# A hybrid mixing and MoE layer step: expert outputs summed in PSUM, scaled selections, nine staged weight slots

## The reference, cut to what matters

```python
x = x + mix
x = x + moe(rmsnorm(x, norm_ffn_g), w_router, b_router, w_up, b_up, w_down, b_down)
...
gu = xb @ w_up[e] + b_up[e]
gate, up = gu[:, :D_EXPERT], gu[:, D_EXPERT:]
act = (up + 1.0) * (gate * jax.nn.sigmoid(SWIGLU_ALPHA * gate))
return act @ w_down[e] + b_down[e]
...
y = jax.ops.segment_sum(out * row_gate[:, None].astype(out.dtype), row_tok, num_segments=n_tok)
```

## Time and profile before

| what | value |
|---|---|
| median of 3 runs | 1290.15 us (1289.37 to 1290.32) |
| span of the profiled execution (the only time given for it) | 1288.5 us |
| PE busy | 1174.2 us (91%) |
| DVE busy | 605.2 us (47%) |
| POOL busy | 467.4 us (36%) |
| ACT busy | 249.7 us (19%) |
| moved by DMA | 448.97 MB, 348 GB/s over the span |

### The profile page before, as it was taken

One profiled execution on the slowest core, in us unless ns is written; L12 is line 12 of the kernel. 1 busy time (PEld: TensorE's weight loads), 2 busy tenths in 40 slices (PEclk: granted clock), 3 DMA queues, 4 the chain that ended last, 5 costly groups with the idle time before them and its releaser, 6 DMA issues.

```text
span 1288.5 us, 30593 instructions
## 1 busy us (share of the span) xinstructions
PE 1174.2 (91%) x11113; PEld 577.5 (45%) x11114; DVE 605.2 (47%) x1256; ACT 249.7 (19%) x487; POOL 467.4 (36%) x833
## 2 busy tenths in 40 slices
PE   8999999999999899798979998989989799899876
PEld 7777777775434333233323433433333233233232
DVE  2999983122644344354343442444524244444243
ACT  2012124001222122122212221212211122122112
POOL 1022300000444435445451454454444444535451
PEclk9999999999999999999989999999999999999997
DMA  9983442344899999999998799999999999999996
GB/s 260 337 269 119 144 135 105 129 155 166 334 385 399 421 421 422 421 421 421 422 421 364 307 398 422 420 422 421 422 421 421 421 421 421 422 421 408 421 421 254
DMA packets 94570, 448.97 MB, mean 348 GB/s; under 512 B 8526, under 2 KB 42894, under 8 KB 45339
## 3 DMA queue, kind: packets, MB, share of 16 engines
q1 hardware_dynamic: 93742, 446.55, 86.5%
q10 hardware_dynamic: 749, 1.19, 0.3%
q0 software_dynamic: 48, 0.85, 0.2%
HBM read 447.00 MB, written 2.42 MB: 349 GB/s over the span
## 4 chain that ended last, share of the span: by engine, by line
PE 55%; DMA 15%; DVE 13%; POOL 6%; issue 6%; SPq 3%; ACT 1%; DVEq 0%; POOLq 0%; ACTq 0%
PE banks L1369 20%; DMA ring<-in_w_down 15%; PE banks L1379 12%; DVE R L800 8%; PE banks L1164 8%; POOL ring L530 6%; PE banks L1086 4%; PE banks L1144 3%; PE banks L1123 2%; PE banks L1280 2%; SPq L398 1%; PE banks L1130 1%; PE banks L1153 1%; DVE R L809 1%; DVE R L812 0%
## 5 line engine op out<-in xcount | busy, mean ns | idle before, releaser
L1369 PE MATMUL banks<-ring,hT 128*32 128x512 f32 x3328 | 430.4, 611 | 62.3 <-POOL ring L530 57.5
L530 POOL COPY ring<-big 128x512 f32<-128x512 f32 x248 | 146.9, 641 | 554.4 <-SPq L404 554.4
L530 POOL COPY ring<-R 128x512 f32<-128x512 f32 x496 | 289.9, 631 | 113.4 <-DMA R<-in_w_up 113.4
L321 DVE TENSOR_TENSOR xt<-xt,banks 128x1024 f32<-128x1024 f32 x106 | 128.7, 1215 | 403.7 <-PE banks L1144 403.7
L1379 PE MATMUL banks<-ring,hT 128*32 128x256 f32 x3328 | 227.4, 392 | 18.4 <-DMA ring<-in_w_down 13.2
L1379 PEld LDWEIGHTS banks<-ring,hT 128*32 128x32 f32 x3328 | 107.5, 113 | 202.8 <-issue 123.3
L1164 PE MATMUL banks<-hT,ring 128*128 128x288 f32 x768 | 189.2, 407 | 0.2 <-ACT hT L554 0.2
L1369 PEld LDWEIGHTS banks<-ring,hT 128*32 128x32 f32 x3328 | 95.5, 111 | 195.6 <-POOL ring L530 81.1
L1164 PEld LDWEIGHTS banks<-hT,ring 128*128 128x128 f32 x768 | 145.7, 191 | 39.9 <-issue 0.3
L680 ACT COPY WT<-banks 128x256 f32<-128x256 f32 x52 | 19.4, 373 | 498.2 <-PE banks L1379 498.2
L800 DVE SCALAR_TENSOR_TENSOR R<-big,convw,R 128x256 f32<-128x256 f32 x240 | 108.1, 525 | 0.0
(11 more groups left out here) (252 smaller groups left out, 757.2 us busy)
## 6 DMA issues: line engine op xcount, KB each, us to landing
ring<-in_w_down SPq DMA_DIRECT2D x128, 1024.0 KB, 11.0
R<-in_w_up SPq DMA_DIRECT2D x124, 1024.0 KB, 18.1
ring<-in_w_up SPq DMA_DIRECT2D x70, 1024.0 KB, 9.4
big<-in_w_up SPq DMA_DIRECT2D x62, 1024.0 KB, 12.7
ring<-in_w_in SPq DMA_DIRECT2D x24, 1024.0 KB, 10.3
ring<-in_w_branch_b SPq DMA_DIRECT2D x4, 1024.0 KB, 4.9
ring<-in_w_branch_a SPq DMA_DIRECT2D x4, 1024.0 KB, 4.9
ring<-in_w_out SPq DMA_DIRECT2D x4, 1024.0 KB, 4.9
```

Of the source, the lines that this page charges most:

```text
L321: nc.vector.tensor_tensor(dst, dst, rows, ALU.add).then_inc(y_added, 1)
L530: ins = nc.gpsimd.tensor_copy(ring[:, k, h * 512:(h + 1) * 512], parked[k][:, h * 512:(h + 1) * 512])
L1369: ins = mm(UP[g * BLK:(g + 1) * BLK, :], xT[:, k, :], ring[:, k, g * 512:(g + 1) * 512], start=k == 0, stop=k == UP_SLOTS - 1)
```

## The change

It does five things.

- The sums of all expert outputs for rows 0 to 255 stay in four PSUM banks (`total`) from the first item to the last. `clear_total` opens them once with matmuls of zeros before the loop; every combine accumulates (`start=False`), and DVE adds the two totals to `xt` once after the loop. The last item's output still goes the old way (`tail_out`). The sample rows are added per body as before.
- PE gathers from `xt` itself; the selections carry each row's scale instead of 1. The scaled copy in `stage` goes. The sum of squares of rows 0 to 255 comes from statistics on DVE (`bn_stats`, `bn_aggr`) instead of a square on ACT.
- The buffers of the mixing part move into one region, `arena`, laid out so that nine parked slots fit: up 0 to 7 and the first down slot.
- Before the loop SP loads five parked slots once the spatial gating has been taken out of PSUM (`sp_evac`), a sixth after the first four slots of the first expert, two after `ya_evac` and the ninth at the end.
- In the loop SP releases nine slots, loads three directly, and takes turns in another order (`next_weights`). POOL makes 36 copies per expert instead of 24.

Constants for the order of experts are made on POOL after the convolution instead of near the start, in a buffer that is free only then. The diff, cut to its core:

```diff
-PARKED = 6
+PARKED = 9
+EARLY_SLOTS = 5
+ARENA = PARKED * SLOT + D
...
+        arena = sb("arena", [P, ARENA])
+        parked = [arena[:, k * SLOT:(k + 1) * SLOT] for k in range(PARKED)]
+        stage = region(NT * D).rearrange("p (t d) -> p t d", t=NT)
+        spb = region(G * P).rearrange("p (g i) -> p g i", g=G)
+        big = region(KC * CB)
...
+        region(EARLY_SLOTS * SLOT - taken[0])
+        R1, R2, R4, R3 = (region(KC * T) for _ in range(4))
+        fing = arena[:, PARKED * SLOT:PARKED * SLOT + D]
...
+        zeros = comb[:, 0].rearrange("p q j -> p (q j)")
...
-        row_out = (high[:, :, 0:256], high[:, :, 256:512])
+        total = (high[:, :, 0:256], high[:, :, 256:512])
...
+            def wait_used(k, before):
                 if k < UP_SLOTS:
+                    sp.wait_ge(up_used, before * UP_SLOTS + (k + 1))
                 else:
+                    sp.wait_ge(down_used, before * DOWN_SLOTS + (k - UP_SLOTS + 1))
+            def release_parked(before, ks):
+                for k in ks:
+                    wait_used(k, before)
                     sp.sem_inc(released, 1)
+            def load_direct(e, before, ks):
+                for k in ks:
+                    wait_used(k, before)
                     load_slot(e, k)
...
+            sp.wait_ge(sp_evac, 2 * G)
+            sp.wait_ge(v_stored, 16)
+            for k in range(EARLY_SLOTS):
+                load_parked(1, k)
             for k in range(UP_SLOTS):
                 sp.wait_ge(*mix_block_used(MIX_BLOCKS - SLOTS + k))
                 load_slot(0, k)
+                if k == 3:
+                    load_parked(1, EARLY_SLOTS)
             sp.wait_ge(ya_evac, 2 * KC)
-            for k in range(PARKED - 1):
+            for k in range(EARLY_SLOTS + 1, PARKED - 1):
                 load_parked(1, k)
             for k in range(UP_SLOTS, SLOTS):
                 sp.wait_ge(*mix_block_used(MIX_BLOCKS - SLOTS + k))
                 load_slot(0, k)
             load_parked(1, PARKED - 1)
             sp.wait_ge(before_known, 1)
+            def next_weights(place, here, after, before):
+                release_parked(before, range(0, 3))
+                load_parked_again(place + 1, after, (0,))
+                release_parked(before, (3,))
+                load_parked_again(place + 1, after, (1,))
+                release_parked(before, (4,))
+                load_parked_again(place + 1, after, (2,))
+                release_parked(before, (5, 6))
+                load_parked_again(place + 1, after, (3,))
+                release_parked(before, (7,))
+                load_parked_again(place + 1, after, (4,))
+                release_parked(before, range(UP_SLOTS, PARKED))
+                load_direct(here, before, range(PARKED, SLOTS))
+                load_parked_again(place + 1, after, range(5, PARKED))
             with sp.Fori(1, NE - 1) as place:
                 before = sp.value_load(items_before[0:1, bass.ds(place - 1, 1)], min_val=0, max_val=MAX_ITEMS)
                 here = sp.value_load(order[0:1, bass.ds(place, 1)], min_val=0, max_val=NE - 1)
                 after = sp.value_load(order[0:1, bass.ds(place + 1, 1)], min_val=0, max_val=NE - 1)
-                release_parked(before)
-                load_up_rest(here, before)
-                load_parked_again(place + 1, after, range(0, 2))
-                load_down(here, before)
-                load_parked_again(place + 1, after, range(2, PARKED))
+                next_weights(place, here, after, before)
             before = sp.value_load(items_before[0:1, NE - 2:NE - 1], min_val=0, max_val=MAX_ITEMS)
             here = sp.value_load(order[0:1, NE - 1:NE], min_val=0, max_val=NE - 1)
-            release_parked(before)
-            load_up_rest(here, before)
-            load_down(here, before)
+            release_parked(before, range(PARKED))
+            load_direct(here, before, range(PARKED, SLOTS))
...
-                nc.scalar.activation(stage[:, tt, :], xt[:, tt, :], ACT.Square, accum_out=ss[:, tt:tt + 1]
...
-                for tt in range(NT):
-                    ins = V.tensor_scalar(sel[:, tt, :], slot_ids[:, bass.ds(rank0, BLK)],
-                                          rankm[:, tt, bass.ds(expert, 1)], None, ALU.is_equal)
-                ins.then_inc(sel_ready, 1)
+                for tt in range(2):
+                    V.tensor_scalar(sel[:, tt, :], slot_ids[:, bass.ds(rank0, BLK)],
+                                    rankm[:, tt, bass.ds(expert, 1)], ss[:, 4 + tt:5 + tt], ALU.is_equal, ALU.mult)
+                V.tensor_scalar(sel[:, 2, :], slot_ids[:, bass.ds(rank0, BLK)],
+                                rankm[:, 2, bass.ds(expert, 1)], None, ALU.is_equal).then_inc(sel_ready, 1)
...
+                dve.wait_ge(x2_ready, 2 * tt + h + 1)
+                link(V.bn_stats(bnst[:, tt, h, :], dst))
+                if h == 1:
+                    link(V.bn_aggr(mv[:, tt, :], bnst[:, tt, :, :]))
+                    V.scalar_tensor_tensor(ss[:, tt:tt + 1], mv[:, tt, 0:1], mv[:, tt, 0:1], mv[:, tt, 1:2],
+                                           ALU.mult, ALU.add).then_inc(squared2, 1)
...
-                if tt < 2:
-                    V.tensor_scalar(stage[:, tt, :], xt[:, tt, :], col2, None, ALU.mult).then_inc(rows_kept, 1)
...
-            dve.wait_ge(combined, 1)
-            add_output(dve, row_out[0], 0)
...
-            def add_before(i, tt):
-                dve.wait_ge(combined, i * NT + (tt + 1))
-                add_output(dve, row_out[tt], tt) if tt < 2 else add_quarters(dve, DN[:, 256:512])
+            def add_before(i):
+                dve.wait_ge(combined, i + 1)
+                add_quarters(DN[:, 256:512]).then_inc(y_added, 1)
             with dve.Fori(0, bodies) as i:
                 column, column1, column2 = (
...
                 activate(i, column)
                 take_x(i + 1)
                 swish(i)
-                add_before(i, 2)
+                add_before(i)
                 dve.wait_ge(combT_turned, i + 1)
                 select_weighted(column1)
                 dve.wait_ge(gathered, i + 2)
                 select(column2)
-                add_before(i, 1)
-                dve.wait_ge(combined, i * NT + (NT + 1))
-                add_output(dve, row_out[0], 0)
...
-            add_before(bodies, 2)
-            add_before(bodies, 1)
+            add_before(bodies)
+            for tt in range(2):
+                add_rows(total[tt], tt).then_inc(total_added, 1)
...
-                    mm(XB[q * BLK:(q + 1) * BLK, 0:256], sel[:, tt, :], stage[:, tt, q * 256:(q + 1) * 256],
+                    mm(XB[q * BLK:(q + 1) * BLK, 0:256], sel[:, tt, :], xt[:, tt, q * 256:(q + 1) * 256],
...
+            def clear_total():
+                for q in range(QN):
+                    row = slice(q * BLK, (q + 1) * BLK)
+                    mm(high[:, q, :].rearrange("p (h n) -> p h n", h=2), zeros[row, :],
+                       slot_ids[row, 0:256].unsqueeze(1).to_broadcast([BLK, 2, 256]), start=True, stop=False)
-                             out_sb[q * BLK:(q + 1) * BLK, :], start=True, stop=True)
+                             out_sb[q * BLK:(q + 1) * BLK, :], start=start, stop=stop)
...
-                pe.wait_ge(y_added, i * NT + 1)
-                combine(1, row_out[1])
+                combine(1, total[1], False, stop)
...
                     pe.wait_ge(listed, 1)
+                    clear_total()
                     tr(DN[0:1, 0:P], item_column).then_inc(list_turned, 1)
...
-            combine(0, row_out[0])
+            combine(0, total[0], False, False)
...
-                combine_before(i)
+                combine_before(i, False)
                 turn_weights(i)
                 pe.wait_ge(xT_ready, i + 2)
                 for k in range(UP_SLOTS):
                     up(k, after)
                     if k == 1:
                         pe.wait_ge(act_ready, i + 1)
-                        pe.wait_ge(y_added, i * NT + 2)
+                        pe.wait_ge(y_added, i + 1)
                     if 1 <= k <= DOWN_SLOTS:
                         down(k - 1, here)
                     if k == 6:
                         pe.wait_ge(combT_ready, i + 2)
                         pe.wait_ge(out_ready, i + 1)
-                        pe.wait_ge(y_added, i * NT + NT)
-                        combine(0, row_out[0])
+                        combine(0, total[0], False, False)
...
-            pe.wait_ge(y_added, bodies * NT + NT)
+            pe.wait_ge(total_added, 2)
...
```

More of the change, by code:

```diff
@@ L134, in hybrid_layer, with region @@
-        rank_at = sb("rank_at", [NE, NE - FIXED])
-        movable = sb("movable", [NE, 1])
-        first_place = sb("first_place", [NE, 1])
-        big = sb("big", [P, KC * CB])
-        R1 = sb("R1", [P, KC * T])
-        R2 = sb("R2", [P, KC * T])
-        R3 = sb("R3", [P, KC * T])
-        R4 = sb("R4", [P, KC * T])
+        stageq = sb("stageq", [P, 256])
+        fingq = sb("fingq", [P, 256])
```

(57 more changed lines are left out.)

126 lines of the change are left out of this document (49 added, 77 removed).

## The result

The changed kernel takes 1366.84 us (median of 4 runs, 1363.16 to 1370.85) against 1289.76 for the kernel before: a ratio of 1.0602, interval [1.0586, 1.0618]. It is slower by 77 us. The prediction said 1280.4 and gave "slower" a chance of 0.10.

A forecast was written before the change was run, and what follows sets the result against it. The prediction took the DMA stream of expert weights as the bound. Its terms, -7.5 - 3.6 - 1.5 + 0.4 + 2.5 = -9.7 us, gave span 1278.8 and time 1280.4 us, range 1266 to 1288.

The forecast's parts named there:

- POOL beside DVE: DVE's activation work under POOL's longer copying: one slower body per expert, five experts pay; +2.5 us, bounds 0 and 8.
- rival C: Four DVE operations of the activation chain each wait out one whole copy: 1.6 us a body, time 1285.9; chance 0.08.
- Only the five experts in the stretches that PE holds pay: Part of the +2.5 us for DVE under copies: the slower body costs time only where PE holds the stream back.
- Rival D: Between turned rows and first down, a 2.5 us delay in every body makes PE the bound: 1300; chance 0.06.
- Rival B: SP's loads: late POOL copies hold up every load behind them, gaps grow and the gain goes: 1290; chance 0.10.
- Start of the stream: The loop's first load waits only for POOL's copy of slot 0, so bytes flow from 336.8: -3.6 us.
- Gaps: Stream runs dry at direct loads in early cycles and around the three-block expert: losses 20.2 against 21.7, -1.5 us.
- Last byte: End of the weight stream: the last byte lands at 1260.1, 12.6 us earlier.
- Adds, clearing, routing, selections: Adds removed from DVE, totals cleared on PE, routing statistics on DVE, scaled selections: 0 each, clearing's 1.3 us counted in cycles.
- The end: Work behind the last weight byte: nothing is shortened; +0.4 us, at most +0.9, at least 0.

The follow-up runs named there:

- the ninth run: The changed kernel, with POOL waiting for its own copies after the third and sixth slot of an expert only; 1282.50 us, 0.9949 of the kernel before.
- the fourth run: The changed kernel, with DVE's multiply for the next block's xT moved ahead of the clamp of the gate; 1346.01 us, 1.0430 of the kernel before.
- the third run: The changed kernel with six slots staged, not nine, and the old order of loads, the rest kept; 1289.17 us, 0.9998 of the kernel before.

## Why the prediction was wrong

**The step that failed is "POOL beside DVE": +2.5 us, bounds 0 and 8.** It took its price from the one body of the earlier trace rows whose activation lay under copies, 0.5 us, and its upper bound from one whole copy per conflict (rival C). Both assume that DVE gets its turn when a copy ends. The body seen had 13 copies behind its clamp, which was 0.58 us long:
```profile
344.01 0.58 DVE L1026 TENSOR_SCALAR hT<-hT 128x256 f32<-128x256 f32 x1
```
It was not the only one: 26 of that kernel's 52 clamps begin under a copy, most behind 1 to 4, and none takes over 0.77 us. The price of a short wait was about right; but no clamp of the kernel before stood behind 15 copies or more. The 36 copies of the changed kernel brought 21 to 25 behind the clamp of 20 bodies, and there the turn came at the end of the chain. The step measured 84.3 us (the changed kernel less the ninth run).

By the Trainium skill (SBUF — State Buffer, "Who interferes with whom"), VectorE in a two-port mode and GpSimd contend, and whichever issues first holds the shared ports for its whole instruction while the other blocks. The short waits, of one copy at most, agree; the long ones, through up to 24 further copies, go beyond it, and there the measurement decides. The same section says that a VectorE instruction with one SBUF input, outside the two-port modes, does not contend: L800 of the fourth run, at 0.41 to 0.43 us under copies, agrees.

**"Only the five experts in the stretches that PE holds pay" failed with it.** A late first down holds back the direct loads whatever slack the expert has: the gaps recur to the end of the loop. Rival D had the place (between the turned rows and the first down) but put the wait into every body at 2.5 us; it was 4 to 5.5 us in 20 of 52, and its 1300 was 67 short. Rival B named what came, gaps that grow, but by way of late copies; the loads that came late (535.55) waited for PE's second down.

**The other steps hold, as the ninth run shows, where the chains are broken.**
- Start of the stream: 282 GB/s from 336 to 338 is 1.3 us' worth, so bytes flow from 336.7 (predicted 336.8).
- Gaps: 3.7, 2.2, 2.0 in the first three cycles (3.7, 2.2, 1.7), then 6.7, 4.1 and 1.9 around the three-block expert (6.9, 4.0, 1.7). Each is its window's length times what it lacks of 421.5 GB/s. No gap follows 760, as predicted.
- Last byte: 172 GB/s in 1260 to 1262 puts it at 1260.8 (1260.1).
- Adds, clearing, routing, selections: 0 in sum (the third run).
- The end: +0.4 predicted, +2.9 measured. In the ninth run the four last downs end 6.8 us behind the last byte, before the change 3.9. The chain of waits of that run shows why:
```profile
1255.54 2.32 POOL ring L556 x4
1257.90 1.11 PE banks L1406 x8
...
1263.93 3.66 PE banks L1416 x64
```
The copy of the last up slot ends at 1257.86, not at 1255.9 as the prediction's terms would have it (landed 10.0 before this last byte, seen 2.8 later, copied in 2.3): POOL works the slots off in order and is behind the landings. All four downs then wait for the activation.

The ninth run's profiled span is 1279.0, against 1278.8 in the prediction's sum. The match is partly luck: 2.5 of that sum, for POOL beside DVE, stands where the end's 2.5 turned up, and the profiled execution is the fastest of five (their median, 1282.50, is 2.1 above the forecast). Staging nine slots is worth 6.7 us (from the third run's 1289.17 to 1282.50) as long as POOL lets go of the ports.

## What to carry to other kernels

A short wait seen once beside another engine bounds nothing when the change lengthens that engine's work: ask what the wait becomes when the other engine never pauses, and price the case. Where GpSimd copies in a long row beside short VectorE operations on the path, make it wait for its own copies every dozen instructions: two waits of 0.14 us an expert were worth 84 us here. Look for the loss at the wait's last consumer: it was paid in DMA's idle time, two engines away from the clamp.

## What the runs showed of the hardware

- A VectorE `tensor_scalar` from SBUF to SBUF (0.29 us) that met a row of GpSimd copies waited for one copy at most behind 13 copies or fewer, counted since GpSimd's last pause (as defined above). Behind 15 or more it waited on through the row: for copies of 512 columns to the row's end (up to 6.74 us, behind 24), for copies of 256 to the row's end or until 42 to 44 copies had run (up to 8.76 us, behind 16). The border lies between 13 and 15 for 512 columns and between 8 and 16 for 256; rows of 1024 columns stayed open at 13, and none was longer at a clamp. One clamp behind 24 copies got in after 0.55 us. What counts the copies is not known.
- A VectorE multiply that reads PSUM and one SBUF operand kept its 0.41 us under the same copies.
- The recorded length of the copies from the new region grows by 6 ns from one to the next (0.62 to 0.79 us over 32), that of the old buffers does not (0.61 to 0.62). It is not the cause of the waiting, and 32 bytes of offset don't change it; its own cause is open.
